# Expert stage: gate and up rows of two experts taken unit by unit in turn, and a fourth pair of weight half buffers

## The reference

```python
def swiglu(t, wg, wu, wd):
    return (jax.nn.silu(t @ wg) * (t @ wu)) @ wd
# moe_swiglu: 8 experts, 1024 -> 1408 -> 1024, each token uses its best 2
vals, idx = lax.top_k((t @ router), 2); gates = softmax(vals)
out = sum_e combine[:, e:e+1] * swiglu(t, wg[e], wu[e], wd[e])
```

## Time and profile before

| | |
|---|---|
| three runs | 1652.3, 1654.03, 1657.71 us |
| the profiled execution | 1657.36 us, of it 1655.6 us in the span |
| PE busy in the span | 1604.3 us, 97% |
| PE weight loads | 1450.6 us, 88% |
| DVE, ACT, POOL busy | 74%, 59%, 34% |
| DMA moved | 339.76 MB, mean 205 GB/s |
| the expert stage | about 1236 to 1640 us of the span, some 100 us a pair |

### The profile page before, as it was taken

The page is one execution under the profiler, slowest core; times in us unless marked ns, Lnnn a source line. Parts: engine busy times, 40 slices in busy tenths (PEclk is TensorE's granted clock), DMA queues, the critical chain, the costliest instruction groups (busy, mean ns, idle before and its releaser), DMA issues.

```text
span 1655.6 us, 27908 instructions
## 1 busy us (share of the span) xinstructions
PE 1604.3 (97%) x10996; PEld 1450.6 (88%) x10996; DVE 1218.1 (74%) x1751; ACT 980.2 (59%) x1419; POOL 566.3 (34%) x439
## 2 busy tenths in 40 slices
PE   7999999999999999999999999999999999999997
PEld 6988888898888889998999999999997878777786
DVE  6565776656567656898875554799987797988887
ACT  6556675446657634555554443555557777777775
POOL 1231552123217501143120002132137648566571
PEclk9999999999999999999999999999999999999999
DMA  8632455555335554543435455543529999999982
GB/s 288 230 119 103 164 193 192 181 200 183 112 132 198 179 202 178 177 148 117 164 124 185 176 179 179 169 153 128 179 85 354 330 367 327 369 335 342 359 331 78
DMA packets 50775, 339.76 MB, mean 205 GB/s; under 512 B 5639, under 2 KB 7903, under 8 KB 11439
## 3 DMA queue, kind: packets, MB, share of 16 engines
q1 hardware_dynamic: 47920, 328.79, 55.7%
q0 software_dynamic: 2720, 9.13, 1.8%
HBM read 336.76 MB, written 1.13 MB: 204 GB/s over the span
## 4 chain that ended last, share of the span: by engine, by line
PE 82%; ACT 7%; DVE 5%; issue 3%; POOL 1%; DMA 0%; DVEq 0%; ACTq 0%; SPq 0%; POOLq 0%
PE bank L581 12%; PE bank L555 9%; PE bank L557 8%; PE bank L556 8%; PE bank L579 7%; ACT wh L1345 5%; PE bank L1000 3%; PE bank L712 3%; PE bank L1002 3%; PE bank L1001 3%; PE bank L714 3%; PE bank L713 3%; DVE wl L1915 2%; PE bank L1008 2%; PE bank L1009 2%
## 5 line engine op out<-in xcount | busy, mean ns | idle before, releaser
L1915 DVE TENSOR_TENSOR wl<-stg,wh 128x2048 fp32r<-128x2048 f32 (+1 forms) x266 | 605.1, 2283 | 209.3 <-ACT wh L1345 209.2
L1345 ACT ACTIVATE wh<-stg 128x2048 fp32r<-128x2048 f32 x266 | 507.4, 1910 | 129.4 <-PE bank L1002 44.3
L555 PE MATMUL bank<-xx,wh 128*128 128x272 f32 (+1 forms) x778 | 225.5, 290 | 0.0
L557 PE MATMUL bank<-xx,wl 128*128 128x272 f32 (+1 forms) x778 | 223.3, 287 | 0.0
L556 PE MATMUL bank<-xx,wh 128*128 128x272 f32 (+1 forms) x778 | 223.1, 287 | 0.0
L2883 POOL TENSOR_TENSOR wl<-stg,wh 128x256 fp32r<-128x256 f32 x88 | 170.5, 1943 | 109.8 <-ACT wh L1345 109.8
L581 PE MATMUL bank<-xx,wh 128*128 128x512 f32 x448 | 159.6, 396 | 0.0
L581 PE MATMUL bank<-H,wh 128*128 128x512 f32 x434 | 151.3, 390 | 0.0
L556 PEld LDWEIGHTS bank<-xx,wh 128*128 128x128 f32 x778 | 147.5, 190 | 0.0
L555 PEld LDWEIGHTS bank<-xx,wh 128*128 128x128 f32 x778 | 146.3, 188 | 1.1 <-issue 0.7
L557 PEld LDWEIGHTS bank<-xx,wl 128*128 128x128 f32 x778 | 146.3, 188 | 0.0
(11 more groups left out here) (435 smaller groups left out, 4106.0 us busy)
## 6 DMA issues: line engine op xcount, KB each, us to landing
stg<-in_w SPq DMA_DIRECT2D x178, 1024.0 KB, 4.9
stg<-in_units SPq DMA_DIRECT2D x86, 1024.0 KB, 5.5
sq<-in_units SPq DMA_DIRECT2D x22, 1024.0 KB, 5.9
stg_more<-in_units SPq DMA_DIRECT2D x20, 1024.0 KB, 5.4
BT<-bias_scratch POOLq DMA_DIRECT2D x3, 1024.0 KB, 10.3
BT<-bias_scratch POOLq DMA_DIRECT2D x1, 2048.0 KB, 12.8
BB<-bias_scratch POOLq DMA_DIRECT2D x2, 1024.0 KB, 6.3
stg<-in_tails SPq DMA_DIRECT2D x4, 512.0 KB, 4.2
```

Of the source, the lines that this page charges most:

```text
L555: pe.matmul(out, wh, xh(kt), start=kt == 0, stop=False)
L557: ins = pe.matmul(out, wl, xh(kt), start=False, stop=kt == KT - 1)
L1345: act.activation(WH[u % NW][:, :], stg[stage_of(u)][:, :], ACT.Copy).then_inc(*m.inc("w_high", u))
L1915: vec.tensor_tensor(WL[u % NW][:, 0:n], stg[stage_of(u)][:, 0:n], WH[u % NW][:, 0:n].bitcast(F32), ALU.subtract).then_inc(*m.inc("w_low_v" ...
```

## The change

- One stage buffer fewer (`MORE` 2 to 1, so 5 in the expert stage) and a fourth pair `WH`/`WL` from unit `RING_FROM` = 183 on. `ring_of(u)` says which pair a unit uses, `last_in_ring(u)` which unit was there before it (u-4 instead of u-3).
- G exists once instead of twice. The four `gather` of the next pair move from between the rows of gi = 1 and 2 into the down stage (after the big units n = 1 to 4).
- The rows of a pair are ordered by `phases(j, gi)`: first all gate rows of both experts, then all up rows, each by unit, one unit of big and one of few in turn. The first group of the first pair keeps the old order. The DMA order of the units follows.
- `turn` of big moves: from behind the gate rows of few of the same gi to behind row 2 of the *next* group (after unit 0's third row), or behind the second down step for the last group. `turn_and_sum` of few moves from behind row 2 of big to behind row 2 of few of the next group (`hook` (0,1,1) in the down stage). The halves of both (`high`, `low`, `small_gate`, `small_high`, `small_hidden`, `small_low`) move with them.
- `hidden_of` of big on DVE is called after all rows of the up phase, so behind the conversions that belong to few's last unit too. Before, it was called after big's own up rows.
- The second arm of the program (every expert on all tokens) is changed alike. It does not run with these inputs.

The diff, cut to its core:

```diff
-MORE = 2
+MORE = 1
-PAIR_UNITS = [(s, 4 * gi + n) for gi in range(2) for s in range(2) for n in range(4)] + ...
+LATER_UNITS = [(s, n) for n in range(16) for s in range(2)] + [None]
+PAIR_UNITS = [[(s, n) for s in range(2) for n in range(4)] + LATER_UNITS[8:]] + [LATER_UNITS] * 3
+def ring_of(u):
+    if u < RING_FROM:
+        return u % NW
+    k = (u - RING_FROM) % (NW + 1)
+    return NW if k == 0 else (RING_FROM + k - 1) % NW
+def last_in_ring(u):
+    return u - NW if u < RING_FROM else u - NW - 1
+def phases(j, gi):
+    n0, nn = GU[gi]
+    every = [(s, up, kt) for s in range(2) for up in range(2) for kt in range(KD)]
+    if j == 0 and gi == 0:
+        return [every[KD * i:KD * (i + 1)] for i in range(4)]
+    by_unit = lambda r: ((2 * KD * n0 + (r[1] * KD + r[2]) * nn) // UT, r[0], r[2])
+    return [sorted([r for r in every if r[1] == up], key=by_unit) for up in range(2)]
...
# TensorE
-                        rows("sp", big, gi, 0, [large], "gate_sp", ...)
-                        if gi > 0 and j < PAIRS - 1:
-                            gather(j + 1, 2 * gi - 2)
-                        rows("sp", big, gi, 1, [large], "hidden_sp", nothing, nothing)
-                        rows("sp", few_, gi, 0, [small_], "gate_rows", ...)
-                        turn("sp", big, gi, 0, 0)
-                        rows("sp", few_, gi, 1, [small_], "up_rows", nothing, nothing)
+                        for i, phase in enumerate(phases(j, gi)):
+                            for s, up, kt in phase:
+                                one_row(s, gi, up, kt)
+                                if gi > 0 and (s, up, kt) == (0, 0, 2):
+                                    turn("sp", big, gi - 1, 0, mtm2[0])
+                                if gi > 0 and (s, up, kt) == (1, 0, 2):
+                                    turn_and_sum(few_, gi - 1)
...
                     def hook(n, s, i_step):
                         if (n, s, i_step) == (0, 0, 1):
+                            turn("sp", big, 2, 0, mtm2[0])
+                        if (n, s, i_step) == (0, 1, 1):
                             turn_and_sum(few_, 2)
+                        if 0 < n < 5 and (s, i_step) == (0, 3) and j < PAIRS - 1:
+                            gather(j + 1, n - 1)
...
# Splits (ACT and DVE)
             def enter(self, u):
-                while self.made < min(u + NW, N_UNITS) and not self.held:
+                while self.made < N_UNITS and last_in_ring(self.made) < u and not self.held:
                     self.split(self.made)
+            def row(self, j, gi, s, up, kt):
+                ...  # counts the tiles used of each unit
+                while self.used.get(self.low) == UT:
+                    self.low += 1
+                self.at += nn
+                self.enter(self.low)
...
# VectorE
+                        for i, phase in enumerate(phases(j, gi)):
+                            for s, up, kt in phase:
+                                sp.row(j, gi, s, up, kt)
+                                if gi > 0 and (s, up, kt) == (1, 0, 0):
+                                    low(big, gi - 1)
+                                if gi > 0 and (s, up, kt) == (0, 0, 6):
+                                    small_hidden(few_, gi - 1)
+                                if gi > 0 and (s, up, kt) == (1, 0, 7):
+                                    small_low(few_, gi - 1)
+                            if (0, 1, KD - 1) in phase:
+                                hidden_of("sp", big, gi, 0, mtmp[0], mtm2[0], last)
```

More of the change, by code:

```diff
@@ L1010, in in_two @@
                 return product
[L1012 to L1032, removed]
-                                ins.then_inc(*m.inc(f"group_{tag}", ("unit", u)))
-                    at[0] += nn
-                    each(kt)
@@ L1037, in turn, with row @@
-            def turn(tag, x, gi, i, j):
+            def row(tag, j, s, gi, up, kt, products, read, operand):
+                x, (n0, nn) = 2 * j + s, GU[gi]
+                first = 2 * KD * n0 + (up * KD + kt) * nn
+                if kt == 0:
+                    for i in range(len(products)):
+                        b, old = bank((tag, "gu", x, gi, up, i), (read, (x, gi, i)))
+                        held.add(b)
+                        vacant(old)
+                operand(kt)
+                pieces = [(unit_of(j, s, n), k, c, o) for n, k, c, o in pieces_of(first, nn)]
+                for i, product in enumerate(products):
+                    b = m.bank[tag, "gu", x, gi, up, i]
+                    for pi, (u, k, c, o) in enumerate(pieces):
+                        if k == 0:
+                            unit_ready(u)
+                        ins = product(PS[b][:, o * P:(o + c) * P], kt, WH[ring_of(u)][:, k * P:(k + c) * P], WL[ring_of(u)][:, k * P:(k + c) * P])
+                        over = i == len(products) - 1 and k + c == UT
+                        if kt == KD - 1 and pi == len(pieces) - 1:
+                            ins.then_inc(*m.inc(f"group_{tag}", ("gu", x, gi, up, i)))
+                            if over:
+                                m.also(f"group_{tag}", ("unit", u))
+                            let_go(b)
+                        elif over:
+                            ins.then_inc(*m.inc(f"group_{tag}", ("unit", u)))
+                at[0] += nn
@@ L1039, in turn @@
+            def turn(tag, x, gi, i, hidden):
                 nn = GU[gi][1]
@@ L1799, in sparse @@
-                        if gi > 0 and j < PAIRS - 1:
-                            gather(j + 1, 2 * gi - 2)
-                        for kt in range(KD):
-                            sp.run(nn)
-                        gate_of("sp", big, gi, 0, 0, prev)
-                        if gi > 0 and j < PAIRS - 1:
-                            gather(j + 1, 2 * gi - 1)
-                        for kt in range(KD):
-                            sp.run(nn)
-                        rows_out(few_, gi, 0)
-                        high(big, gi)
@@ L1890, in scalar_program @@
                 sparse()
-            sp.at, sp.made, w.seen = state[0], state[1], dict(state[2])
+            sp.at, sp.made, sp.used, sp.low, w.seen = state[0], state[1], {}, 0, dict(state[2])
             m.count["w_high"] = sp.made
@@ L2533, in gates, with hidden_of @@
                 in_order(SHARE[:, :, :], cm, step).then_inc(*m.inc("combine_" + tag, 0))
-            def hidden_of(tag, x, gi, i, j, prev):
+            def hidden_of(tag, x, gi, i, gate, dst, last):
                 n = GU[gi][1] * P
```

281 lines of the change are left out of this document (141 added, 140 removed).

## The result

The changed kernel takes **1702.29 us** (median of 4 runs, 1701.16 to 1702.69) against 1653.16 us (1651.81 to 1657.71) for the kernel before on the same chip: 1.029 times as long, 95% interval 1.027 to 1.0312. It is slower by 49 us; 1682 was predicted, with a range up to 1700. The profiled run took 1701.16 us, 43.8 more than the profiled run of before.

The account below looks back on a forecast made before the run. The prediction took PE's own in-order work to bound the kernel, with 24.1 us lost in waits. Its terms, -11.9 + 31.1 + 9 = +28 us on 1654, gave 1682 us; 8 of 10 runs were to lie from 1661 to 1700.

Parts of the forecast that it names:

- The forecast of eleven waits: PE at `turn`: eleven or twelve waits for DVE's multiplication, 3 to 4 us each, some 40 us in all.
- Part 3: PE's clock: stretches at half clock behind the new waits of `turn`, +9 us, from a range of 0 to 18.8.
- The bound of 18.8 us: Upper end for the clock's cost: eleven waits, each followed by a slow stretch of 3.41 us that costs 1.7.
- Part 2: `turn` and the product in front of it: longer waits on PE, 43.3 us against 12.2, so +31.1 us (24.5 to 36.6).
- part 4: Edits costed at nothing: one stage buffer fewer, gathers in the down stage, Silu and halves of the hidden values moved.
- Part 1: Fourth pair of halves and even order: PE's 21 waits for weights or few's copied rows all go, -11.9 us.
- The ceiling: PE's waits in the stage, corrected, sum to 24.1 us, so a perfect order could bring 24 us and no more.
- the one with a fall after every wait and DVE further behind: Rival: clock falls after every wait, DVE one conversion further behind, +43.5 us, so 1698 us; chance 0.15.

Follow-up runs that it names:

- e1: The changed kernel with big's `hidden_of` on DVE called ahead of the conversions that the last up rows release: 1633.48 us, ratio 0.987.
- e4b: The changed kernel with 7, 9 or 12 matmuls of constants put in front of eleven of the transposes: 1678.27 us, ratio 1.0148.
- e12: The changed kernel with `hidden_of` between the conversion released by big's last up unit and those released by few's: 1656.95 us, ratio 1.0022.
- e7: The changed kernel with three pairs of half buffers instead of four, all else kept: 1727.06 us, ratio 1.043.
- e16: The changed kernel with `small_high` on ACT behind row 2 of few's up rows and `small_low` on DVE behind `hidden_of`: 1694.64 us, ratio 1.0231.
- e11: The changed kernel with the old order of rows and units and three pairs of halves instead of four: 1662.1 us, ratio 1.0048.
- e3: The changed kernel with the old order of rows and units, few's work moved to fit, four pairs kept: 1633.48 us, ratio 0.9873.
- e14: e1 with four stage buffers instead of five: 1649.76 us, ratio 0.9972.
- e17: The changed kernel with `hidden_of` ahead of the last conversions in the last group of each pair only: 1671.25 us, ratio 1.0093.
- e4: The changed kernel with 14, 19 or 25 matmuls of constants put in front of eleven of the transposes: 1723.5 us, ratio 1.0411.
- e15: e1 with DVE making all 2048 columns of each low half in the expert stage, GpSimd none: 1632.69 us, ratio 0.9878.

## Why the prediction was right in its sign and too small

**The mechanism was right.** The product stands behind the conversions of few's last unit, `turn` stands still for it, and all else on PE behind `turn`: e1 takes just that away and all the loss with it. The forecast of eleven waits came out too; they are 48.6 us and not some 40, and a pair takes 112.8 us where some 107 was said.

**Part 3 failed: the clock.** It was put at +9 us, and it is +24 (e4b; some 19 net of what the kernel before already lost by such stretches, at most 5.1 us). Two assumptions were wrong. That each stretch would be 3.41 us long, because the one of before was the earlier trace rows: eight of eleven are 6.83. And that half of a stretch would fall into the wait: 18.8 of 64.9 us do. The bound of 18.8 us was thus no bound: it was taken from a single row, where the waits that it was to hold for were two to three times as long. The stage of before had a second stretch, of 6.83 us, at its start, which the working left out:

```profile
1238.26:1245.08 6.82, 6.82 (x21) 5.56 (x21) 3.29 (x5) 1.73 (x4) 2.57 (x1) 0.50 1.01 426
```

The Trainium skill (TensorE: Matmul & The Clock Gate, section "HAM oscillation — how this bites in real kernels") has the clock down again after each wait between bursts, and the trace of the change agrees: 11 of 11. It isn't so for every wait of this case: none of the seven of 1.0 to 1.8 us in e12 has half clock behind it, nor has one of 3.12 us in e7. For waits as long as the change's, taking half of the 18.8 us was the wrong choice.

**Part 2 was mis-sized: +31.1, measured +38.2** (48.6 + 11 x 0.16 = 50.4, less 12.2). The first two waits were right: 3.5 and 4.0 were said, 3.0 to 3.6 and 4.2 came. The third was 5.6, not 4.2. The working counted two conversions ahead of the product; there were four in a row, and they began late, because ACT had stood still for few's product (e16, where the four begin earlier: 1.2 us of the 1.4). I had written that the halves of the hidden values move but are not needed until the down stage. That is true of who needs them and says nothing of who stands queued behind them. So this edit of part 4, costed at nothing, has a price of some 8 us.

**Part 1: -11.9, measured -7.4** (3.4 + 7 x 0.16 = 4.5, from 11.9). The assumption that all of these waits go was a little too good. Not all of the 21 were for weights or copied rows either: four (1.1 us) were for few's hidden halves (`SHB`), and for four (1.7 us) the profile names nothing; they are gone too. But as a measure of the fourth pair it says little: with the product on time the fourth pair is worth 28.6 to 41.6 us. The kernel before has three pairs and loses only 11.9 to such waits. e11, its order and ring with the change's other edits, is 8 us slower than it. Which of those edits costs the 8 us (the stage, the single G, the later `turn`) wasn't tried one by one, so this stays open.

**The ceiling held in the medians, partly by luck.** I wrote that a perfect order could bring 24 us and no more, the sum of PE's waits. e1 and e3 bring 21, but e1 still waits for 6.6 us in the stage (18.8 before): some 5 of the 21 are the half clock of before, which the ceiling left out. Between the profiled runs e1 brings 24.8 us.

**The rest of part 4 shows no cost with four pairs.** e1 has five stages and the gathers in the down stage, and PE waits there for weights for 3.9 us only (with one stage fewer it costs 16 us, e14). Neither was taken back by itself, so a small price isn't excluded.

**The sum.** 38.2 - 7.4 + 23.0 - 5.1 = +48.7 us, measured +43.8 in the profiled runs and +49.1 in the medians. The 5 us between 48.7 and 43.8 are spread over all terms. Counted from start to start of PE's matmuls in both traces (an estimate: 1238 to 1640 us before, 1238 to 1684 after), the gaps that are too short for the list of waits are 2.6 us less, the half clock makes the matmuls 15.8 us longer in all and not 17.9, and the waits grow by 30.2 us and not 30.8. Of the rivals, the one with a fall after every wait and DVE further behind (1698 us) was the nearest. It had a chance of 0.15 because it needed two things at once; both happened, the second at the third waits alone, and they aren't independent, since a DVE further behind makes the waits longer.

## What to carry to other kernels

On an engine with an in-order program, bulk work that is made ahead should stand *behind* the short result that another engine is about to wait for; see what the chain shows just before the waiting instruction, and count every bulk operation that can be queued there, also those that a third engine delivers late. A wait of the matrix engine can cost half as much again as it lasts: here 50 us of waits brought 24 us lost to half clock. When a change holds a gain and a loss together, take them apart before judging it: this one is 3% slower as a whole and 1.3% faster with one call moved.

## What was unexpected of the hardware

- All eleven waits of the change, 2.95 us and more, were followed by half clock, for 3.41 or 6.83 us. The four of 5.6 us all had 6.83; of the seven others four had 6.83 and three 3.41, in no order of their length, and in e17, where the third waits are gone, the same seven had 3.41 each. Of the shorter waits, 1.66 us was followed by it (in the kernel before), while 1.77 and 1.71 us (e12) were not, and nor was 3.12 us in e7, with the clock at 1.00 in the wait and for 15 us behind it. The length of a wait alone doesn't decide. In e7, `turn` in the timeline, then the window behind it:

```profile
1284.14 0.63 PE L1076 MATMUL bank<-consts,xc 128*128 128x128 f32 x4 [3.12 <-DVE xc L2587]
...
1284.14:1299.60 15.46, 11.25 (x74) 10.76 (x74) 7.33 (x6) 9.59 (x9) 7.01 (x3) 1.00 0.74 267
```

- A float32 matmul of constants with 256 columns runs as two matmuls of 0.216 us on the engine (e4).
- GpSimd's eighth is worth nothing: DVE needs 2.23 us a conversion beside it, 2.29 for all columns alone (e15). The Trainium skill (SBUF — State Buffer, section "Who interferes with whom") calls the shared port an exclusive lock; these two numbers agree with it.
